# Half of the columns of each conditioning piece to TensorE in four column tiles, half to VectorE, instead of whole pieces to one of the two

## The reference

```python
c_act = jax.nn.silu(c)
mod = c_act @ w_ada[l] + b_ada[l]                       # (2048) @ (2048 x 12288)
sh1, sc1, g1, sh2, sc2, g2 = [m[:, None, :] for m in jnp.split(mod, N_MOD, axis=-1)]
h = rms_norm(x, norm1_w[l]) * (1.0 + sc1) + sh1
proj = h @ w_in[l]                                      # (256 x 2048) @ (2048 x 7168)
...                                                     # attention, HGRN2
x = x + g1 * (concat(y_attn, y_rec) @ w_out[l])
h = rms_norm(x, norm2_w[l]) * (1.0 + sc2) + sh2
...                                                     # gated conv FFN, final norm
```

## Time and profile before

| | |
|---|---|
| median of 3 runs | 1305.28 us |
| profiled execution, span from first to last instruction | 1303.5 us |
| TensorE busy | 1265.0 us, 97% |
| VectorE busy | 998.9 us, 77% |
| ScalarE busy | 600.8 us, 46% |
| DMA, bytes moved | 329.77 MB, 253 GB/s on average |
| chain that ended last | 88% TensorE, 4% VectorE, 3% DMA, 2% ScalarE |

### The profile page before, as it was taken

How to read it: one execution, slowest core, us unless ns; L and a number is a source line. 1 busy time by engine, 2 the same in 40 slices (tenths; PEclk the granted TensorE clock), 3 DMA queues, 4 the chain that set the end, 5 groups by cost and what they waited for, 6 DMA issues and landing times.

```text
span 1303.5 us, 20846 instructions
## 1 busy us (share of the span) xinstructions
PE 1265.0 (97%) x7302; PEld 1117.9 (86%) x7302; DVE 998.9 (77%) x1297; ACT 600.8 (46%) x795; POOL 51.3 (4%) x99
## 2 busy tenths in 40 slices
PE   5899899999999999999999999999999999999997
PEld 5888899998998878888888888888888888888886
DVE  4788698998998989787978797888767766545454
ACT  3335454444546644454444444444444444434342
POOL 0000200022121000000000000000000000000000
PEclk9789899999999999999999999999999999999999
DMA  9999788788789899758777777777666676555553
GB/s 338 387 386 351 268 307 273 260 272 278 245 285 307 279 343 376 264 176 290 235 236 239 241 228 241 238 236 216 192 193 192 181 267 214 193 194 194 193 193 114
DMA packets 156067, 329.77 MB, mean 253 GB/s; under 512 B 11493, under 2 KB 20438, under 8 KB 155106
## 3 DMA queue, kind: packets, MB, share of 16 engines
q1 hardware_dynamic: 152352, 318.49, 73.4%
q0 software_dynamic: 3360, 9.98, 2.3%
q10 hardware_dynamic: 290, 0.44, 0.1%
HBM read 323.09 MB, written 4.19 MB: 251 GB/s over the span
## 4 chain that ended last, share of the span: by engine, by line
PE 88%; DVE 4%; DMA 3%; ACT 2%; issue 2%; SPq 0%; DVEq 0%; ACTq 0%
PE bank L1217 23%; PE bank L1225 12%; PE bank L1280 6%; PE bank L1282 6%; PE bank L1281 6%; PE bank L959 5%; PE bank L961 5%; PE bank L960 5%; PE bank L946 4%; PE bank L948 4%; PE bank L949 4%; DMA pc<-in_w_ada 3%; DVE acc_c L1375 2%; PE bank L980 1%; PE bank L993 1%
## 5 line engine op out<-in xcount | busy, mean ns | idle before, releaser
L640 ACT ACTIVATE whi<-wraw 128x1024 fp32r<-128x1024 f32 x408 | 425.0, 1059 | 601.4 <-PE bank L1225 228.9
L1363 DVE TENSOR_TENSOR wlo<-wraw,whi 128x1024 fp32r<-128x1024 f32 x404 | 491.4, 1222 | 245.0 <-ACT whi L640 243.4
L1217 PE MATMUL bank<-h,whi 128*128 128x512 f32 x1400 | 334.7, 391 | 1.1 <-DVE h L1625 0.8
L1217 PEld LDWEIGHTS bank<-h,whi 128*128 128x128 f32 x1400 | 257.1, 188 | 51.7 <-issue 1.2
L1225 PEld LDWEIGHTS bank<-h,wlo 128*128 128x128 f32 x1400 | 179.6, 191 | 6.9
L1225 PE MATMUL bank<-h,wlo 128*128 128x256 f32 x1400 | 181.7, 283 | 0.0
L946 PE MATMUL bank<-h,whi 128*128 128x256 f32 x512 | 148.5, 290 | 5.5 <-DVE h L1388 5.5
L948 PE MATMUL bank<-h,whi 128*128 128x256 f32 x512 | 145.7, 285 | 0.0
L949 PE MATMUL bank<-h,wlo 128*128 128x256 f32 x512 | 145.7, 285 | 0.0
L1280 PE MATMUL bank<-whi,act_hi 128*128 128x512 f32 x336 | 131.0, 390 | 0.0
L1281 PE MATMUL bank<-wlo,act_hi 128*128 128x512 f32 x336 | 130.8, 389 | 0.0
(11 more groups left out here) (240 smaller groups left out, 1336.0 us busy)
## 6 DMA issues: line engine op xcount, KB each, us to landing
wraw<-in_w_up SPq DMA_DIRECT2D x176, 512.0 KB, 3.8
araw<-in_w_ada SPq DMA_DIRECT2D x128, 512.0 KB, 5.4
wraw<-in_w_in SPq DMA_DIRECT2D x112, 512.0 KB, 4.8
wraw<-in_w_down SPq DMA_DIRECT2D x88, 512.0 KB, 3.7
pc<-in_w_ada SPq DMA_DIRECT2D x48, 512.0 KB, 11.5
wraw<-in_w_out SPq DMA_DIRECT2D x32, 512.0 KB, 6.2
pc<-in_w_ada SPq DMA_DIRECT2D x32, 256.0 KB, 7.2
x<-in_x SPq DMA_DIRECT2D x2, 1024.0 KB, 7.7
```

The lines of the kernel that those rows point to most:

```text
L640: act.activation(whi[:, slot], wraw[:, slot], ACT.Copy).then_inc(s_hi, 1)
L1217: pe.matmul(ps[bank0 + f], whi[:, (ph.unit0 + j) % RING, k, f * P:(f + 1) * P], h[:, kk].rearrange("p a t -> p (a t)"), start=(kk == 0), s ...
L1363: dve.tensor_tensor(wlo[:, slot], wraw[:, slot], whi[:, slot].bitcast(F32), ALU.subtract).then_inc(s_lo, 1)
```

## The change

All 16 pieces of a chunk now go to both engines. Of `sh1` and of `sc1`, TensorE takes the first half of the chunk's columns and VectorE the second half. VectorE's operation is the same on half as many columns (128 x 512, or 128 x 256 in the short chunks), 16 times a chunk instead of 12 or 13.

TensorE's side is turned round: the weights are now silu(c) of 128 rows, as column 0 of a 128 x 32 tile whose other 31 columns are zero (`csil32`), and half of the piece moves past it, 512 columns (or 256) in float32. Piece r writes to the partitions of column tile r mod 4 of bank 6 (`tile_position`), four pieces make a batch, and four batches a chunk. So the sums lie in four rows of the bank. ScalarE copies the bank to `rowsum` (`chunk_rows`), and `chunk_columns` adds over the partitions: the tiles of VectorE's accumulator first, then those of `rowsum`, as many matmuls as before in all.

`load_first` now waits for both engines before it loads a place again. The tables `PE_TILES` and `PE_AFTER` give way to `ROWS_AFTER`; `LOWS_AT`, `LOADS_AT` and `SUM_AFTER` stay.

```diff
-PE_TILES = ((2, 5, 8, 11), (2, 5, 8, 11), (2, 7, 12), (3, 7, 11), (3, 7, 11))
-PE_AFTER = ((0, 1, 3, 4), (0, 1, 3), (0, 1, 3), (0, 1, 1))
+ROWS_AFTER = ((1, 2, 3, 4), (1, 2, 3, 4), (1, 2, 3, 4), (0, 0, 1, 1))
...
             def load_first(i):
                 if i >= PC_RING:
-                    if i - PC_RING in PC_OF_PE:
-                        sp.wait_ge(s_pcp, PC_OF_PE.index(i - PC_RING) + 1)
-                    else:
-                        sp.wait_ge(s_pcd, PC_OF_DVE.index(i - PC_RING) + 1)
+                    sp.wait_ge(s_pcp, i - PC_RING + 1)
+                    sp.wait_ge(s_pcd, i - PC_RING + 1)
...
+            act.wait_ge(s_csil32, 1)
+            act.activation(csil32[:, :, 0], ps[0][:, 0:16], ACT.Silu).then_inc(s_csil32, 1)
...
+            def chunk_rows(c):
+                n = CHUNK[c]
+                act.wait_ge(s_pcp, (c + 1) * KT)
+                if c:
+                    act.wait_ge(s_red, c)
+                act.activation(rowsum[:, :, 0:n // 2 * P], ps[6][:, 0:n * P].rearrange("p (a t) -> p a t", a=2), ACT.Copy).then_inc(s_rows, 1)
...
+            chunk_rows(0)
             for v in range(LATER):
                 first_hi(v)
+                if v + 1 in U0[1:CHUNKS]:
+                    chunk_rows(U0.index(v + 1))
                 for n in range(CHUNKS):
                     if v == U0[n] + 1:
                         chunk_hi(n)
...
-            def first_piece(i):
...
+            def first_rows(c, batch):
+                n = CHUNK[c]
+                if c and batch == 0:
+                    pe.wait_ge(s_rows, c)
+                for r in range(4 * batch, 4 * batch + 4):
+                    i, q = c * KT + r, r % 4 * 32
+                    pe.wait_ge(s_pc[i % PC_RING], (i // PC_RING + 1) * 16)
+                    pe.matmul(ps[6][q:q + 32, 0:n * P], csil32[:, r, :], pc[:, i % PC_RING, :, 0:n // 2 * P], start=(batch == 0),
+                              stop=(batch == 3), skip_group_check=True, tile_position=(0, q)).then_inc(s_pcp, 1)
             def chunk_columns(c):
-                pe.wait_ge(s_pcd, sum(i < (c + 1) * KT for i in PC_OF_DVE))
...
+                n = CHUNK[c]
+                pe.wait_ge(s_pcd, (c + 1) * KT)
+                if c:
+                    pe.wait_ge(s_redc, c)
+                for part in range(2):
+                    for tile in range(n // 2, n):
+                        k = part * n + tile
+                        pe.matmul(ps[7][:, k:k + 1], acc_c[:, c % 2, part, tile * P:(tile + 1) * P], ones[:, 0:1], start=True, stop=True)
+                pe.wait_ge(s_rows, c + 1)
+                for part in range(2):
+                    for tile in range(n // 2):
+                        k = part * n + tile
+                        last = pe.matmul(ps[7][:, k:k + 1], rowsum[:, part, tile * P:(tile + 1) * P], ones[:, 0:1], start=True, stop=True)
                 last.then_inc(s_red, 1)
```

More of the change, by code:

```diff
@@ L74 @@
 LOWS_AT = ((2, 4, 8, 11, 15, 15), (2, 4, 8, 11, 15, 15), (2, 4, 8, 11, 15, 15), (5, 10, 15))
-PC_OF_PE = [c * KT + r for c in range(CHUNKS) for r in PE_TILES[c]]
-PC_OF_DVE = [i for i in range(CHUNKS * KT) if i not in PC_OF_PE]
 OUT0, UP0 = PROJ_UNITS, PROJ_UNITS + 32
@@ L235, in build @@
         acc_c = at(Z + 94 * K, "acc_c", [2, 2, CT * P])
+        csil32 = at(Z + 102 * K, "csil32", [KT, 32])
+        rowsum = at(Z + 76 * K, "rowsum", [2, CT // 2 * P])
         htmp0 = at(Z + 48 * K, "htmp0", [4, SEQ])
@@ L330, in build @@
         s_pcp = sem("s_pcp")
+        s_rows = sem("s_rows")
+        s_csil32 = sem("s_csil32")
         s_pcd = sem("s_pcd")
@@ L546, in _ @@
             st = Steps(gp, s_p)
+            gp.memset(csil32[:], 0.0).then_inc(s_csil32, 1)
             gp.memset(ones[:], 1.0).then_inc(s_cst, 1)
@@ L911, in chunk_columns @@
-            def chunk_columns(c):
-                pe.wait_ge(s_pcd, sum(i < (c + 1) * KT for i in PC_OF_DVE))
[L914 to L917, removed]
+            def first_rows(c, batch):
[7 more added lines that the diff above has]
+                              stop=(batch == 3), skip_group_check=True, tile_position=(0, q)).then_inc(s_pcp, 1)
@@ L918, in chunk_columns @@
                 last.then_inc(s_red, 1)
-            pe.wait_ge(s_csilu, 1)
-            first_piece(2)
+            pe.wait_ge(s_csil32, 2)
+            first_rows(0, 0)
             for k in range(KT // 2):
@@ L931, in _ @@
                 last.then_inc(s_xT, 1)
-            first_piece(5)
-            first_piece(8)
-            first_piece(11)
+            for batch in range(1, 4):
+                first_rows(0, batch)
             chunk_columns(0)
@@ L1158, in _ @@
                     m = max(m for m in range(CHUNKS) if U0[m] <= u)
-                    for r, at_ in zip(PE_TILES[m + 1], PE_AFTER[m]):
+                    for batch, at_ in enumerate(ROWS_AFTER[m]):
                         if u - U0[m] == at_:
-                            first_piece((m + 1) * KT + r)
+                            first_rows(m + 1, batch)
                     if u - U0[m] == SUM_AFTER[m]:
@@ L1367, in first_piece @@
                 dve.wait_ge(s_pc[i % PC_RING], (i // PC_RING + 1) * 16)
-                a, new = acc_c[:, c % 2, :, 0:CHUNK[c] * P], pc[:, i % PC_RING, :, 0:CHUNK[c] * P]
+                cols = slice(CHUNK[c] // 2 * P, CHUNK[c] * P)
+                a, new = acc_c[:, c % 2, :, cols], pc[:, i % PC_RING, :, cols]
                 if r == 0:
@@ L1373, in first_piece @@
                 else:
-                    dve.wait_ge(s_pcd, PC_OF_DVE.index(i))
+                    dve.wait_ge(s_pcd, i)
                     ins = dve.scalar_tensor_tensor(out=a, in0=new, scalar=csilu[:, r:r + 1], in1=a, op0=ALU.mult, op1=ALU.add)
@@ L1378, in chunk @@
             def chunk(c):
-                n, cols, sums = CHUNK[c], slice(CH0[c], CH0[c + 1]), ps[6 + c % 2]
+                n, cols, sums = CHUNK[c], slice(CH0[c], CH0[c + 1]), ps[7]
                 dve.wait_ge(s_red, c + 1)
@@ L1398, in _ @@
             for r in range(KT):
-                if r not in PE_TILES[0]:
-                    first_piece(r)
+                first_piece(r)
                 if r == 1:
@@ L1417, in _ @@
                 for r in range(KT):
-                    if r not in PE_TILES[c + 1] and r >= CHUNK[c] // 2:
+                    if r >= CHUNK[c] // 2:
                         first_piece((c + 1) * KT + r)
```

## The result

The changed kernel takes 1314.56 us (median of 4, 1313.79 to 1316.28) against 1305.51 us (1304.61 to 1307.68) for the kernel before on the same chip: ratio 1.0066, 95% interval 1.0052 to 1.008, slower. The forecast was 1316 us in a range of 1307 to 1331. The profiled execution took 1313.79 us with a span of 1312.0, 8.5 us more than before. The mark of the forecast, TensorE's start on unit 20, moved from 139.60 to 148.33 us, by 8.7: all the time is lost before that mark.

A forecast was written before the change was run, and what follows sets the result against it. TensorE was taken as the bound after 144 us, so early-stage delay reaches the end. Span 1303.5 plus 11.2 us at unit 20 gives 1314.7, with 1.8 around it 1316 us; range 1307 to 1331 us.

The forecast's parts named there:

- own case: TensorE's batches overlap partly, five steps, 2.15 us each; unit 20 starts 11.2 us later, 1316 us in all; chance 0.42.
- rival B: TensorE's four column tiles all run together, 0.86 us a long batch; unit 20 +5.0 us, 1310 us; chance 0.28.
- What bounds, and that nothing is given back later: TensorE's later waits total at most 7.2 us, so delay at 144 us moves the end by the same amount.
- ScalarE's order, the term I rested on: Chunk ends: two high parts queue behind ScalarE's copy; 4.4 to 4.9 us to the factors, 5.9 to chunk 4's sums.
- The second pass of a tile runs beside the first of the next, five steps: TensorE's new matmuls: neighbouring tiles overlap by one pass, giving 2.15 us a long batch, 1.08 in short chunks.
- rival C: TensorE's tiles do not overlap, 3.44 us a long batch; unit 20 +29 us, 1335 us; chance 0.17.
- Change-over: TensorE switching between column tiles and whole array: counted at nothing, at most some 0.2 us a batch.
- R of chunk 4 moves as much, so I count that nothing: Unit 22's load some 7 us later, chunk 4's pieces behind it; TensorE's last batch there equally late, so no cost.
- The clock: TensorE's clock around chunks 3 and 4: streaming matmuls against longer waits, counted at nothing, with -3 to +4 us.
- Rival D: Early stage not slower: sums over halves end earlier, given full overlap, stream and clock; -1 us, 1304 us; chance 0.06.

The follow-up runs named there:

- both moves: Changed kernel with ScalarE's copy behind the two high parts and the first batch of chunk 4 before unit 18: 1305.56 us, ratio 0.9996 to the kernel before.
- kernel before with the load: Kernel before, with SyncE issuing the load of unit 25's weights before the first araw load: 1305.51 us, ratio 0.999 to the kernel before.

## Why the prediction was right, and where it wasn't

The sign, the place and the size came out, but the size by errors against each other: that 1316 lies so near 1314.56 is luck. The mark beside the forecast's two ledgers (own case, and rival B with all tiles together), times in us:

| | own case | rival B | measured |
|---|---|---|---|
| one long batch | 2.15 | 0.86 | 0.86 + 0.35 |
| unit 6 starts | 76.0 | 73.6 | 73.93 |
| unit 12 starts | 106.6 | 104.0 | 103.99 |
| last batch of chunk 3 ends | 125.4 | 120.2 | 121.3 |
| unit 18 starts | 133.1 | 127.9 | 129.03 |
| last batch of chunk 4 ends | 143.2 | 136.9 | 141.2 |
| column sums of chunk 4 start | 149.1 | 142.8 | 146.60 |
| unit 20 starts | 150.8 | 144.6 | 148.33 |

- **What bounds, and that nothing is given back later: right.** The mark moved by 8.7 and the span by 8.5 us; the idle time after 155 us is unchanged.
- **ScalarE's order, the term I rested on: right.** I had 4.4 us from the last batch to the factors in chunk 1, 4.9 in chunks 2 and 3, 5.9 to the sums in chunk 4. From the copy's start it is 4.3 us to the end of the factors in chunk 1 (66.87 to 71.14), 4.6 and 4.8 in chunks 2 and 3, and 5.4 to the sums in chunk 4 (141.21 to 146.60), with up to 0.1 ahead of the copy; the step of a piece on 256 columns was 0.57 us and not 0.60. Moving the copy gave all 8.7 us back.
- **"The second pass of a tile runs beside the first of the next, five steps": wrong.** It was the step on which my own case stood, with no row for it. All four tiles run together, as in rival B: the batch of one tile took 3.62 us and that of four tiles 1.07. The two passes of one float32 matmul keep their tile for themselves, but the next tile's don't wait for them. The Trainium skill ("TensorE: Matmul & The Clock Gate", Part 3: Packing small matmuls — row/col tiling) has column tiles run together, 2.38 times faster with three: here eight passes cost as two, four times fewer. Its rule in the same section, that a weight load overlaps running matmuls only where its row group differs, I had taken for rival C, 3.44 us. Here all tiles use all rows, and yet the eight weight loads lie within 0.16 us under the batch's matmuls (52.08): the measurement decides against the rule for these 32-column weights.
- **Change-over, "at nothing, at most some 0.2 us a batch": wrong.** It is about 0.34 us a batch. With four batches between unit 12 and the end of chunk 3 (4 x 0.34 = 1.4 us) it covers the 1.1 us by which 121.3 is later than B's 120.2.
- **"R of chunk 4 moves as much, so I count that nothing" (the late loads): wrong.** From unit 18 the two units, two pairs of batches at 0.87 us and two change-overs are 2.95 + 2.85 + 1.7 + 0.7 = 8.2 us, so TensorE alone would have been through at 137.3 at the full clock. It was through at 141.2, 3.9 us later. Of these, 1.6 are the clock: unit 18 took 4.54 us to the batch at 133.57, not 2.95.

```profile
130.00:133.30 3.30, 3.30 (x17) 3.30 (x17) 2.99 (x6) 0.00 (x0) 0.00 (x0) 0.50 1.01 332
```

The other 2.3 us are pieces that came later, the last at 140.55. I had looked at one load that was late, that of unit 22 (124.10 us, by line 459, 3.6 after the earlier trace rows), and not at who frees the places of `pc`: four places of chunk 4 wait for a batch that stands behind unit 18. SyncE waits 5.1 us for that batch, which the low clock made later still. Moving the batch gave 2.6 us from unit 18 on.
- **The balance.** My own case was 2.5 us above the measured mark, 2.0 at the end of the last batch and 0.5 from there to the sums. I had charged a long batch 1.29 us too much for its overlap and 0.35 too little for its change-over; the late pieces and the clock behind unit 18, both of which I had at nothing, put 3.9 us back. Rival B had the mechanism and missed the mark by 3.7 us, for the change-overs and for pieces later than its own.
- **The clock: counted at nothing within -3 to +4 us; the margin held, the reading was off.** Besides the 1.6 us behind unit 18 it stood at half (0.53) from 144.1 to 154.4 us, 10.3 us instead of 6.9, in part beside TensorE's wait. I had put the low clock of the earlier trace rows down to the one-column matmuls; in the kernel before it was full until 136 us and 0.81 from 136 to 138, so it fell in the wait of 3.68 us ahead of the last sums. The old kernel had a low stretch in chunk 2 as well, 0.72 from 92 to 98 us, where the changed kernel had 1.00. One trace for each kernel doesn't tell how often such a stretch comes, and a mark read from one trace can be off by the 1 to 1.6 us that it cost above.
- **Small misreadings.** TensorE had 17 whole pieces in the kernel before, not 20 (the 7 long and 6 short ones that the sum uses are right). And unit 0 did start later, at 44.77 instead of 44.07 us.
- **Rival D (not slower)** named conditions that came true with both moves: the tiles together, the load of unit 22 at 120.06 us, the clock at 1.00 in 137.2 to 144.1 us; the kernel is then level with the old, though the stream fell below 387 GB/s (329 from 125 to 137 us). It needed another order on ScalarE, which the change did not have.

## What to carry to other kernels

A step that moves work to an idle engine can still cost time by where its hand-over stands in a third engine's program: list what is queued behind the new waiting instruction, and who waits for that. When two engines must both have read a buffer before it is loaded again, look for the later of the two in program order, not for the busier one. And when a repair gives its time back at the mark but not at the end, look at the next wait (here a DMA stream that stood empty behind one load's wait) before calling the change worthless.

## What the runs showed of the hardware that was not expected

- Float32 matmuls with 32 weight columns, 512 moving columns and four different column tiles run fully together: eight passes in 1.07 us, in one column tile 3.62 us; with 256 columns 0.64 us (line 917 at 109.90).
- Between such a batch and matmuls of the whole array about 0.34 us go in addition, with one tile as with four. The Trainium skill ("TensorE: Matmul & The Clock Gate", Part 3: Packing small matmuls — row/col tiling, under The cost: per-tile semaphore tail) gives a tail of 25 + 4.7 ns a tile + 26.3 ns for each semaphore increment; with four of each that is an estimate of 0.15 us, and no run here tells how much of the 0.34 it is.
- The granted clock (1.00 is 2.4 GHz, 0.5 its level of 1.2 GHz) around the last column sums went with what TensorE did before them: 0.53 and 0.50 after waits of 5.43 and 3.91 us (changed kernel, kernel before with the load), 1.00 where batches ran up to the sums. Behind shorter waits it could go either way: after 2.70 and 2.72 us at unit 12 it stayed at 1.00 in one execution and was 0.64 over the next 4 us in another. Four one-column matmuls took about 0.88 us from start to start at the low level and 0.54 at the high one.
